# The embedding's loads, splits and half of its products moved into the last pair of experts

## The reference

```python
ffn = _moe_ffn(x.reshape(bsz * seq, d), router_w[i], router_b[i], exp_w_gu[i], exp_b_gu[i],
               exp_w_down[i], exp_b_down[i]).reshape(bsz, seq, d)
h = DEEPNORM_ALPHA * x + ffn
h = h + jax.nn.sigmoid(h @ ple_gate_w[i]) * (p[i] @ ple_proj[i])
x = _layer_norm(h, ln2_g[i], ln2_b[i])
```

## Time and profile before

| | us |
|---|---|
| median of 3 runs | 3268.94 (3262.03 to 3270.54) |
| the profiled execution | 3267.66 |
| its span | 3266.0 |
| busy: PE / DVE / ACT / POOL | 3103.1 / 2036.6 / 1545.2 / 202.9 |
| mean granted clock of PE | 0.984 of full |

### The profile page before, as it was taken

How to read it: one execution, slowest core, us unless ns; L and a number is a source line. 1 busy time by engine, 2 the same in 40 slices (tenths; PEclk the granted TensorE clock), 3 DMA queues, 4 the chain that set the end, 5 groups by cost and what they waited for, 6 DMA issues and landing times. The chain is left out here.

```text
span 3266.0 us, 47097 instructions
## 1 busy us (share of the span) xinstructions
PE 3103.1 (95%) x18657; PEld 2307.2 (71%) x18657; DVE 2036.6 (62%) x2537; ACT 1545.2 (47%) x1909; POOL 202.9 (6%) x199
## 2 busy tenths in 40 slices
PE   8998899999999999998999999999999999999998
PEld 6876567575757574664668777788877776778886
DVE  6744759484848483573568866666438876566533
ACT  4424437473737373462376355444226537344422
POOL 0000001121212121120000000000000000000000
PEclk9998999999999999999999999999999999999999
DMA  4112249999999999998122211232322221223331
GB/s 153 60 33 95 75 184 375 388 416 401 407 400 408 397 411 405 408 409 358 33 87 73 72 40 46 84 99 95 108 75 82 66 72 32 61 84 97 98 106 62
DMA packets 117303, 600.21 MB, mean 184 GB/s; under 512 B 19183, under 2 KB 22783, under 8 KB 66706
## 3 DMA queue, kind: packets, MB, share of 16 engines
q1 hardware_dynamic: 105442, 580.57, 46.6%
q0 software_dynamic: 11664, 16.89, 2.0%
HBM read 582.10 MB, written 26.28 MB: 186 GB/s over the span
## 5 line engine op out<-in xcount | busy, mean ns | idle before, releaser
L2844 DVE TENSOR_TENSOR wl<-raw,wh 128x2048 fp32r<-128x2048 f32 x166 | 378.3, 2287 | 65.4 <-ACT wh L2756 64.4
L2756 ACT ACTIVATE wh<-raw 128x2048 fp32r<-128x2048 f32 x166 | 318.1, 1917 | 123.5 <-DMA raw<-in_exp_w 66.4
L4784 ACT ACTIVATE w_high<-w_raw 128x1024 fp32r<-128x1024 f32 (+1 forms) x112 | 129.0, 1152 | 302.6 <-PE acc L4756 161.2
L4833 DVE TENSOR_TENSOR w_low<-w_raw,w_high 128x1024 fp32r<-128x1024 f32 (+1 forms) x112 | 150.0, 1339 | 180.0 <-PE ps L4714 94.7
L4736 PE MATMUL ps<-x_high,w_high 128*128 128x512 f32 x640 | 249.1, 389 | 0.0
L4737 PE MATMUL ps<-x_low,w_high 128*128 128x512 f32 x640 | 249.0, 389 | 0.0
L2649 PE MATMUL pu<-wh,Xh 128*128 128x512 f32 x576 | 233.4, 405 | 15.8 <-DVE wl L2844 15.8
L2651 PE MATMUL pu<-wh,Xl 128*128 128x512 f32 x576 | 227.9, 396 | 0.0
L2650 PE MATMUL pu<-wl,Xh 128*128 128x512 f32 x576 | 227.6, 395 | 0.0
L3581 PE MATMUL acc<-x_high,w_high 128*128 128x512 f32 x528 | 218.5, 414 | 1.5 <-ACT hq L3990 1.5
L3582 PE MATMUL acc<-x_low,w_high 128*128 128x512 f32 x528 | 206.5, 391 | 0.0
(11 more groups left out here) (934 smaller groups left out, 7212.9 us busy)
## 6 DMA issues: line engine op xcount, KB each, us to landing
raw<-in_exp_w SPq DMA_DIRECT2D x226, 1024.0 KB, 15.9
more_raw<-in_exp_w SPq DMA_DIRECT2D x84, 1024.0 KB, 17.6
y<-in_exp_w SPq DMA_DIRECT2D x74, 1024.0 KB, 16.2
w_raw<-in_w_in SPq DMA_DIRECT2D x100, 512.0 KB, 3.4
w_raw<-in_w_up SPq DMA_DIRECT2D x80, 512.0 KB, 3.7
w_raw<-in_w_down SPq DMA_DIRECT2D x32, 704.0 KB, 4.0
w_raw<-in_w_out SPq DMA_DIRECT2D x32, 384.0 KB, 3.1
kv_raw<-in_w_mem_kv SPq DMA_DIRECT2D x16, 512.0 KB, 3.7
```

Of the source, the lines that this page charges most:

```text
L2756: nc.scalar.activation(wh[:, m % PARTS, :], piece, ACT.Copy).then_inc(w_high, 1)
L2844: nc.vector.tensor_tensor(wl[:, m % PARTS, :], slot_of(n, m)[0], wh[:, m % PARTS, :], ALU.subtract).then_inc(w_low, 1)
L4833: nc.vector.tensor_tensor(wl[:, u % 2, 0:width(u)], raw_of(u), wh(u), ALU.subtract).then_inc(low_ready, 1)
```

## The change

SP issues the loads of `ple_proj` and `p` between pieces 17 and 18 of the last pair (EMBED_AT), after a wait for `used` 4. ACT and DVE split them within the last unit. PE forms tiles 0 and 1 after chunk 9, 2 and 3 after chunk 10, 4 and 5 after chunk 11, and 6 and 7 within the joins, after k = 1 and 3. In the joins, join k now stands ahead of the transposes of k. The results `e` go into the memory of the dead `y` (`place_y`), and `p`, `v` and their parts into memory of weight slots that are dead by then. The splits of x have a loop of their own on ACT, which waits for `joined_taken` k+1, and on DVE stand behind all joins as before. The branch of the rest waits for more semaphores inside, which are not waited for where it is not entered. The gate's weights wait for `used` 8 of the last unit.

```diff
@@ -2303,6 +2303,8 @@
 HALF = SLOTS // 2
+EMBED_AT = 18
+EMBED_TILES = {9: (0, 1), 10: (2, 3)}
 SCATTERS = WIDE + 2 * (PAIRS - 1)
@@ -2475,6 +2477,10 @@
                                 sp.wait_ge(used, n.at * CHUNKS + (c // 2 - 3))
+                            if n.last and c == EMBED_AT:
+                                sp.wait_ge(used, n.at * CHUNKS + 4)
+                                ple.sync_proj(sp)
+                                ple.sync_p(sp)
                             chunk_in(right if c % 2 else left, c // 2, pair_slot(n, c))
@@ -2494,10 +2500,8 @@
                 ple.sync_y(sp)
-                sp.wait_ge(used, (UNITS - 1) * CHUNKS + 10)
-                ple.sync_proj(sp)
-                ple.sync_p(sp)
-                rest.sync(sp, joined_taken, DT)
+                rest.sync(sp, [(used, UNITS * CHUNKS), (joined_taken, DT), (ple.added, DT), (ple.e_taken, DT)])
+                sp.wait_ge(used, (UNITS - 1) * CHUNKS + 8)
                 for n in range(DT):
@@ -2676,6 +2680,9 @@
                             pair_chunk(n, following, m)
+                            if n.last:
+                                for t in EMBED_TILES.get(m, ()):
+                                    ple.tensor_embedded(pe, t)
                         else:
@@ -2736,10 +2743,14 @@
                 all_units(pe, unit)
+                ple.tensor_embedded(pe, 4)
+                ple.tensor_embedded(pe, 5)
                 for k in range(DT):
+                    join((UNITS - 1) % 2, k)
                     ple.tensor_turn(pe, k)
-                    join((UNITS - 1) % 2, k)
-                rest.tensor(pe)
+                    if k in (1, 3):
+                        ple.tensor_embedded(pe, 6 + k // 2)
+                rest.tensor(pe, [(joined_taken, DT), (ple.added, DT), (ple.e_taken, DT)])
                 ple.tensor(pe)
@@ -2801,6 +2812,9 @@
                     if n.pair:
+                        if n.last:
+                            ple.scalar_p(act)
+                            ple.scalar_proj(act)
                         turned_part(n.at, 1, True)
@@ -2824,13 +2838,14 @@
                 all_units(act, unit)
+                for t in range(4):
+                    ple.scalar_embedded(act, t)
                 for d in (0, 1):
                     weighted(UNITS - 1, (UNITS - 1) % 2, d, True)
-                ple.scalar_p(act)
-                ple.scalar_proj(act)
-                act.wait_ge(joined_taken, DT)
+                for t in range(4, DT):
+                    ple.scalar_embedded(act, t)
                 rest.scalar(act)
-                ple.scalar(act)
+                ple.scalar(act, joined_taken)
 
@@ -2946,6 +2961,8 @@
                     if n.last:
+                        ple.vector_p(dve)
+                        ple.vector_proj(dve)
                         place_back(n)
@@ -3037,8 +3054,6 @@
                         take_joined(k - 1)
-                ple.vector_p(dve)
-                ple.vector_proj(dve)
                 rest.vector(dve)
@@ -3171,15 +3189,20 @@
             self.yt = yt = K.sb(held, "y_tokens", [P, NT, D])
-            self.e = K.sb(held, "e", [P, DT, S])
+            K.sb(held, "more_raw_kept", [P, 2, CW])
+            with ExitStack() as early:
+                self.v_high = K.sb(early, "v_high", [P, DT, PLE], F32R)
             self.high = K.sb(held, "x_high", [P, DT, S], F32R)
             self.low = K.sb(held, "x_low", [P, DT, S], F32R)
+            K.sb(held, "raw_kept", [P, 4, CW])
+            with ExitStack() as split:
+                self.v_low = K.sb(split, "v_low", [P, DT, PLE], F32R)
             self.v_raw = K.sb(held, "v_raw", [P, DT, PLE])
+            with ExitStack() as split:
+                self.p_low = K.sb(split, "p_low", [P, PT, S], F32R)
             self.p_raw = K.sb(held, "p_raw", [P, PT, S])
             self.p_high = K.sb(held, "p_high", [P, PT, S], F32R)
-            self.p_low = K.sb(held, "p_low", [P, PT, S], F32R)
-            self.v_high = K.sb(held, "v_high", [P, DT, PLE], F32R)
-            self.v_low = K.sb(held, "v_low", [P, DT, PLE], F32R)
+        self.e = place_e
         n = len(EMBED_SEMS)
@@ -3201,6 +3224,20 @@
             sp.dma_start(self.yt[:, j, :], self.a["y_rows"][j * P:(j + 1) * P, :]).then_inc(self.y_in[j], 16)
+
+    def tensor_embedded(self, pe, t):
+        nc, acc, p_high, p_low, v_high, v_low = self.nc, self.acc, self.p_high, self.p_low, self.v_high, self.v_low
+        if t == 0:
+            pe.wait_ge(self.p_split_l, 1)
+            pe.wait_ge(self.v_split_l, 1)
+        if t >= 2:
+            pe.wait_ge(self.e_taken, t - 1)
+        for k in range(PT):
+            c = slice(k * P, (k + 1) * P)
+            nc.tensor.matmul(acc[t % 2], v_high[:, t, c], p_high[:, k, :], start=(k == 0), stop=False)
+            nc.tensor.matmul(acc[t % 2], v_high[:, t, c], p_low[:, k, :], start=False, stop=False)
+            mm = nc.tensor.matmul(acc[t % 2], v_low[:, t, c], p_high[:, k, :], start=False, stop=(k == PT - 1))
+        mm.then_inc(self.e_made, 1)
 
@@ -3268,7 +3290,11 @@
 
-    def scalar(self, act):
+    def scalar_embedded(self, act, t):
+        act.wait_ge(self.e_made, t + 1)
+        self.nc.scalar.activation(self.e[:, t, :], self.acc[t % 2], ACT.Copy).then_inc(self.e_taken, 1)
+
+    def scalar(self, act, x_ready):
         nc, acc, norm = self.nc, self.acc, self.norm
@@ -3277,12 +3303,11 @@
 
-        for t in range(DT):
-            act.wait_ge(self.e_made, t + 1)
-            nc.scalar.activation(self.e[:, t, :], acc[t % 2], ACT.Copy).then_inc(self.e_taken, 1)
-            nc.scalar.activation(self.high[:, t, :], self.x[:, t, :], ACT.Copy).then_inc(self.x_split_h, 1)
-            if t in (2, 5):
-                high_part(t // 3)
+        for k in range(DT):
+            act.wait_ge(x_ready, k + 1)
+            nc.scalar.activation(self.high[:, k, :], self.x[:, k, :], ACT.Copy).then_inc(self.x_split_h, 1)
+            if k in (2, 7):
+                high_part(k // 4)
         for n in range(DT):
@@ -3315,8 +3340,9 @@
             nc.vector.tensor_tensor(low[:, k, :], x[:, k, :], high[:, k, :], ALU.subtract).then_inc(self.x_split_l, 1)
-            if k in (3, 6):
-                low_part(k // 3 - 1)
+            if k == 3:
+                low_part(0)
+        low_part(1)
         for n in range(DT):
```

More of the change, by code:

```diff
@@ L2429, in mixture @@
             rest = RestOfExperts(K, ctx, sems[n_own:n_rest], over, over_ready, a["mixture_in"], w, a["exp_b_gu"], spill, x, pu, pd)
-            ple = Embedding(K, ctx, sems[n_rest:], a, x, gain, shift, [pu[:, 0, :], pu[:, 1, :]], [pu[:, 2, :], pu[:, 3, :], pt[:, :]],
+            ple = Embedding(K, ctx, sems[n_rest:], a, x, place_y, gain, shift, [pu[:, 0, :], pu[:, 1, :]], [pu[:, 2, :], pu[:, 3, :], pt[:, :]],
                             pd[:, 0, :], pd[:, 1, :])
@@ L3073, in done, with sync @@
         eng.wait_ge(self.added, EXPERTS * DT + 2)
-    def sync(self, sp, joined_taken, all_joined):
+    def sync(self, sp, through):
         with self.some(sp):
-            sp.wait_ge(joined_taken, all_joined)
+            for semaphore, count in through:
+                sp.wait_ge(semaphore, count)
             sp.dma_start(self.x[:, :, :], self.x_in).then_inc(self.x_loaded, 16)
@@ L3088, in sync, with tensor @@
             self.done(sp)
-    def tensor(self, pe):
+    def tensor(self, pe, through):
         nc, wt = self.nc, self.wt
         with self.some(pe):
+            for semaphore, count in through:
+                pe.wait_ge(semaphore, count)
             pe.wait_ge(self.ones_ready, 1)
@@ L3162, with __init__ @@
 class Embedding:
-    def __init__(self, K, ctx, sems, a, x, gain, bias, acc, bank, mu, spare):
+    def __init__(self, K, ctx, sems, a, x, place_e, gain, bias, acc, bank, mu, spare):
         self.K, self.nc, self.a, self.x, self.acc, self.bank = K, K.nc, a, x, acc, bank
@@ L3215, in tensor @@
         K, nc, x, norm, acc, bank = self.K, self.nc, self.x, self.norm, self.acc, self.bank
-        p_high, p_low, v_high, v_low, wh, wl, high, low = self.p_high, self.p_low, self.v_high, self.v_low, self.wh, self.wl, self.high, self.low
-        def embedded_tile(t):
-            if t == 0:
-                pe.wait_ge(self.p_split_l, 1)
-                pe.wait_ge(self.v_split_l, 1)
-            if t >= 2:
-                pe.wait_ge(self.e_taken, t - 1)
-            for k in range(PT):
-                c = slice(k * P, (k + 1) * P)
-                nc.tensor.matmul(acc[t % 2], v_high[:, t, c], p_high[:, k, :], start=(k == 0), stop=False)
-                nc.tensor.matmul(acc[t % 2], v_high[:, t, c], p_low[:, k, :], start=False, stop=False)
-                mm = nc.tensor.matmul(acc[t % 2], v_low[:, t, c], p_high[:, k, :], start=False, stop=(k == PT - 1))
-            mm.then_inc(self.e_made, 1)
+        wh, wl, high, low = self.wh, self.wl, self.high, self.low
         def tile(n):
@@ L3247, in tile @@
             mm.then_inc(self.product, 1)
-        for t in range(DT):
```

(1 more changed line is left out.)

## The result

The change takes 3272.07 us (median of 20 runs, 3267.03 to 3279.82) against 3267.21 us of before in the same comparison (20 runs): ratio 1.0016, 95% interval 1.0010 to 1.0022. It is slower, clear of the noise, but by only about half of the 0.3% that the prediction called telling. The profiled execution took 3275.72 us and its span is 3274.1 us.

What follows compares the result with a forecast made beforehand. Bounds: the last pair's weight loads, then DVE in the joins. (a) to (d) +3.1 us and (e) +2 sum to +5.1 on 3267.66; against the median 3268.94 that gives 3274 us (+0.16%), range 3262 to 3282.

Steps and rivals of the forecast that it cites:

- (a): Loads ahead of chunks 9 to 11: nine loads fill the queue, so chunk 9 comes 4.1 us later.
- Rival C: Load queue: small loads move at the pace SP issued them, 8.4 us instead of 4.1, giving 3278; chance 0.06.
- (b): PE from chunk 9 to the first join: chunks and tiles take 19.6 us without another wait; splits hidden, price nothing.
- (c): Chunk 9: the low clock after PE's 5.7 us wait costs +1.9 us; ends 0 and +2.8.
- (d): Joins: PE and DVE alternate, 2.54 us a step; first g +3.1 us for (a) to (d) together.
- (e): Joins and gate tile: low clock again, two steps and a bit of the tile, +2 us; ends 0 and +6.6.
- Rival A: Joins keep their pace because something in PE's queue lets transposes pass; 3264 to 3266; chance 0.14.
- Rival B: Clock stays low on chunk 9, all six join steps and the gate tile: +12.6, 3282; chance 0.13.

Runs made afterwards that it cites:

- e4: The kernel before, with only the nine loads moved ahead of piece 18 of the last pair (and the memory they need): 3271.17 us, 1.0016 of before.
- e3: The change, with five matmuls whose result nothing reads in PE's wait ahead of chunk 9: 3267.35 us, 0.9996 of before.
- e1: The change, with the transposes of column k again ahead of join k: 3266.49 us, 0.9995 of before.
- e2: The kernel before, with only join k put ahead of the transposes of column k: 3278.46 us, 1.0031 of before.
- e7: The change, with one matmul whose result nothing reads behind the transposes of columns 3 to 7: 3269.49 us, 1.0005 of before.
- e8: The change's early products, the filled wait ahead of chunk 9, and joins added onto their column's transposes in one of five banks: 3259.57 us, 0.9969 of before.
- e5: The change, with transposes again ahead of each join and five unread matmuls filling the wait ahead of chunk 9: 3263.85 us, 0.9986 of before.
- e9: The kernel before, with only the joins changed, each added onto its column's transposes in one of five banks: 3262.93 us, 0.9989 of before.
- e6: Joins as in e9, with the change's order on ACT, the nine loads behind the last weights and y, all eight tiles behind the joins: 3265.38 us, 0.9999 of before.

## Why the prediction was right, step by step

The prediction put the first g 5.1 us later than before and the median at 3274; it came 5.1 us later, and the ratio of 1.0016 is the predicted +0.16%. The predicted 3274 stood on a median of three runs, the 3272.07 on another sample: against its own 3267.21 the same sum gives 3272.3. The steps hold one by one, with small errors that cancel.

- **(a)** said +4.1 us on chunk 9; e4 and the change show +3.6 (+8.9 instead of +5.3 from chunk 8). PE's wait was 5.27, not 5.7. That 4.1 came so near is in part luck, because the rows were misread. The prediction took v and p to stand behind y_tokens, whose last piece landed at 1539.6, and the time from there to p's landing for what the nine loads need. The trace of before shows v's pieces otherwise:

```profile
L3191 SPq DMA_DIRECT2D v_raw<-in_ple_proj x8: 343/565/2174, 1529.3 to 1534.1; - x8
...
DMA to landing us min/median/max: 4.0/4.2/8.2
```

  The first landed at 1533.3, and seven of the eight by 1538.0, ahead of y's last. A working that holds is an estimate from the bytes: the nine loads are 1.57 MB, and in the change the queue moved 427 GB/s from 1500 to 1507 and from 1517 to 1530, which gives 3.7 us. Between 1507 and 1517, with v's pieces in it, it moved only 302 GB/s; why chunk 9 was no later for that, no run tells. Rival C, loads moving at the pace of their issue, 8.4 us, is excluded by chunk 9's row. So is what the page that spoke for it would make of the time: by the Trainium skill, "DMA: Bandwidth & Descriptors", section "Bandwidth", whose table is for transfers issued from GpSimd, it would be 9.1 us (the prediction's estimate, v's pieces at the 64 KB rate and p at the 1 MB rate), and chunk 9 came 3.6 us later.
- **(b)** said 19.6 us without a gap from chunk 9 to the first join, and a window of 18.1 us with PE busy 18.10 shows it. The whole way took 22.0 us with (c), said 21.5, which makes up for what (a) had too much; the difference lies in chunk 10 with its tiles (6.5 us, said 6.2) and chunk 11 with its (6.4, said 6.2).
- **(c)** said +1.9; e3 shows 1.8, and with it the page named there (the Trainium skill, "TensorE: Matmul & The Clock Gate", section "Loop structure matters more than you think") was borne out. The low clock lasted 6.8 us there, from +5.9 to +12.7, but 3.0 of them passed in the wait itself. And e4 shows what the prediction did not say: the term exists only because the tiles filled the waits for the next weights.
- **(d)** said 2.54 us a step; it is 2.54, and e1 and e2 show that the order of the two calls makes it. The branch, said to end at +21.2 from the first join with 0.8 us to spare, ran from 1566.0 for 3.54 us, to +21.1, and the gate's first matmul is released by x_low. This agreement is partly chance: join 7 came 0.8 us later than (d) had it, in a slow step of (e), and the branch began ahead of the last transposes (1566.45), not behind them. Rival A fell with it.
- **(e)** said +2 us with two slow steps and a bit of the gate's tile. The two steps were there (1.8 us); the bit of the gate's tile was 0, as e7 shows. So the right sum has a bit of luck in it. The low clock itself lasted 13.7 us, which on an engine that never waits would cost half of that, 6.9 us (an estimate); it cost 1.8, since PE stood waiting in a good part of it and x_low's pace on DVE covered the gate's tile. Rival B's condition, half clock already at join 4, was not met: the clock fell at +43.5, behind join 5 (+41.9). That it was near is shown by e2, where the clock fell at join 3 and the first g came 11.6 us late.

From the first join on the sum ran: predicted last sum's end +19.3 and 2 us more for (e), 21.3; measured 21.0.

What stays open: e3's runs, and e8's, were about 0.1% quicker than their traces explain, and no run tells whether something behind the stretch had a part in it or the sample.

## What to carry to other kernels

Where two engines hand banks to each other, the order of two calls on one of them can turn a pipeline into a taking of turns: before work is put into such a stage, write down for each wait what the other engine can do meanwhile. Filling idle time of TensorE with real work has a price where the work's inputs must be loaded for it: loads put ahead of a critical stream cost here what their transfer takes (e4: 3.6 us), and what is moved must win more than that. The move did so once the joins had their old order and the wait ahead of chunk 9 was filled (e5: first g 2.0 us earlier than before). And if two results of TensorE are added anyway, let it accumulate them in one bank: by itself this gained 4.5 us of the stretch (e9), more than the move at its best, and both together gained 6.3 (e8).

## What the runs showed of the hardware

- The branch on PE's queue took 3.3 to 3.6 us in all eleven kernels, while those of ACT and DVE took 0.05 to 0.06. But it isn't always paid. PE's queue ran ahead of matmuls that waited for nothing: in e8 the branch starts at 1558.0 and the last join's first matmul only at 1560.15, and PE then stood only 2.06 us. In the change, where the last join waits for DVE, the branch began at 1566.0, together with that join's second matmul (1566.02). The branch's rows, of the change and then of e8 (ns, start in us):

```profile
L3085 PEldq COMPARE_BRANCH  x1: 3542/3542/3542, 1566.0 to 1566.0; - x1
L3085 DVEq COMPARE_BRANCH  x1: 63/63/63, 1568.9 to 1568.9; - x1
```

```profile
L3084 PEldq COMPARE_BRANCH  x1: 3604/3604/3604, 1558.0 to 1558.0; - x1
```

- Half clock lasted 3.4 or 6.8 us where dense work followed the wait (e1, e6, e9; before, e4, e5), and 10.2 to 23.9 us where PE was busy only in part (e3, the change, e2). So the length went with what stood behind the wait, as far as these runs show: e2's 23.5 us at 0.53 had PE busy 12.59. And in the joins of the change it fell though no wait there was longer than 1.38 us.
- Transposes (float32) and matmuls of float32r accumulated in one PSUM bank, the first transpose starting the bank and everything else adding to it (e6, e8, e9); in e6 and e9 that took 0.9 us a column with no gap.
